# Expert bias as three bf16 parts on 96 rows, made in the banded stage

## The chip, the cores and the metric

One core of one Trainium2 chip runs the whole program. The metric is the device time of one execution in microseconds (us). The granted clock of TensorE has two levels here, 1.2 and 2.4 GHz.

## What is computed

One encoder block on x of 1024 tokens and 1024 columns, all float32, followed by a mixture of experts. What matters here is the second half:

```
logits = xt @ w_router + b_router
top_val, top_idx = lax.top_k(logits, TOP_K)          # 4 of 32 experts
gates = jax.nn.softmax(top_val, axis=-1)
...
gu = xb @ w_gate_up[e] + b_gate_up[e]                # 1024 -> 2 x 1024, bias 32 x 2048
gate = jnp.minimum(gu[:, :D_FF], SWIGLU_LIMIT)
up = jnp.clip(gu[:, D_FF:], -SWIGLU_LIMIT, SWIGLU_LIMIT)
act = (up + 1.0) * (gate * jax.nn.sigmoid(SWIGLU_ALPHA * gate))
y = act @ w_down[e] + b_down[e]
```

Each token's four rows y, times its gates, are added to the residual x; a last RMSNorm gives the output. Before it stand an input projection, stick-breaking attention, sliding window attention and an output projection.

## The kernel before

Float32 products are made of parts. A weight or an activation is split in a high part, rounded to fp32r (ScalarE), and a low part, the rest (VectorE), and TensorE does three fp32r matmuls, high x high, high x low and low x high.

**Stages.** First the norm and its transposes, then the input projection together with stick-breaking attention, ending at about 374 us. Then the **banded stage**: sliding window attention in 32 steps, four to each of the eight tiles of 128 tokens, with the later work of each tile in the same loop at fixed steps behind it, as written out in `out_stage(step)` on VectorE and ScalarE and in `before_turn` and `after_values` on TensorE. `tile_at(step, n)` is the tile whose turn comes n steps after its first step, 4t + n. For tile t VectorE does at 4t + 7 the scaled rows (`mix_rows`, L1781), at 4t + 8 the low parts (`mix_low_part`, L1866), at 4t + 13 the residual (L1801), at 4t + 15 the normed row h2 (`normed`, L1811), at 4t + 18 the routing (L1818 to L1837), at 4t + 20 the places (L1844 to L1860). Beside it runs `band(u + 1)` (L1745, L1749), the scores of the next step, which ScalarE then exponentiates and TensorE turns (L924). Steps 32 to 48 are the tail, without attention.

GpSimd in that stage splits q (L712 to L715), adds the output bias to x (`x2_bias`, L722, at step 4t + 12), takes powers (L646) and writes records of the tokens to their experts' slots by indirect DMAs (L653). SP's queue, per tile t: load x of tile t (L566), then store the residual of tile t - 1 (L569) and h2 of tile t - 1 (L571), each after its semaphore. Behind tile 7 it stores the last two (L575, L577), **loads the bias twice** (L579), and the first weights (L525).

**The bias before.** b_gate_up, 32 experts by 2048 columns, lies on rows 0 to 31 and again on 32 to 63 of `bias_raw`. After the tables of items are started, VectorE adds 1 to the up half (L1934, the "+ 1" of the activation), ScalarE rounds it to fp32r (L1589) into `bias_hl`, VectorE clears rows 64 to 127 (L1973) and makes rows 32 to 63 the rest (L1975, `bias_done`). TensorE and ScalarE wait for `bias_done` before the loop. In the same stretch TensorE turns the first item's gathered rows (L1120), ScalarE makes `x_high` (L1496), VectorE `x_low` (L1969).

**The expert loop**, 33 items, each an expert and up to 192 of its tokens. The first 128 are the stationary operand. TensorE's order for an item: bias of gate and up (`expert_bias`, L1142, two matmuls for each half h of the hidden columns), 8 units of weights for h = 0, 8 for h = 1 (`hidden`, L1152), 8 of the down projection (L1174). A unit is 1024 weight columns, six matmuls of 512 columns. `pick` is a matrix with ones in the rows of the expert, made by GpSimd (`choose`, L766), so that pick x bias_hl puts the expert's bias on every token. Items with more than 128 tokens do the others in plain fp32, in narrow matmuls: 4 groups of 32 tokens' columns for up to 160 tokens, 2 of 64 for more. Their bias is the k = -1 of `over_hidden` (L1186):

```
bias = bias_f.rearrange("p (g h f) -> p h g f", g=2, h=2)
for k in range(-1, KT):
    for q in range(parts):
        lhs = pick_f[:, 0:m] if k < 0 else xo[:, k, 0:m]
        rhs = bias[:, h] if k < 0 else gu_w[:, h, k]
```

Weights are loaded by SP (L525 gate and up, 1 MB for two units; L549 down), refilled as soon as they are split and, in items with extra tokens, used by `over_hidden`. ScalarE makes high parts (L1519), VectorE low parts (L1995), five units ahead at most.

## Time and profile before

| what | value |
|---|---|
| median of 3 runs | 2077.31 us (2076.71 to 2078.88) |
| the profiled execution's own time | 2076.9 us |
| its span, first to last instruction | 2075.1 us |
| TensorE matmul busy | 1955.7 us (94%) |
| VectorE busy | 1579.5 us (76%) |
| ScalarE busy | 1397.3 us (67%) |
| GpSimd busy | 468.7 us (23%) |
| HBM read, written | 472.09 MB, 38.55 MB |
| mean granted TensorE clock | 0.974 of 2.4 GHz |

In the rows below PE is TensorE's matmuls, PEld its weight loads, DVE VectorE, ACT ScalarE, POOL GpSimd, SPq the queue of SyncE. A matmul's recorded time is from its start to its modelled end and overlaps the next one, so its cost is read from one start to the next. `128*32 128x256 f32 x8` is a stationary operand of 128 rows and 32 columns, 256 moving columns, eight instructions. L1186 is line 1186.

### The profile page before, as it was taken

Reading aid. Unit: us, or ns where it says so; the run is one execution under the profiler, and the core shown is the slowest. Engines: PE = TensorE matmul, PEld = TensorE weight load, DVE = VectorE, ACT = ScalarE, POOL = GpSimd, SP = SyncE. Lnnn points to the kernel's source line nnn. Section 1 sums busy time; section 2 is a strip of 40 time slices with the busy share of each in tenths; the row PEclk is TensorE's granted clock in tenths of the full one; section 3 lists DMA queues with packets and bytes.
Section 4 is the critical chain, followed back from the end, with each engine's and each line's share of the span. In section 5 each row is a group of like instructions: output and inputs, shape, how many; then the busy total and the mean of one; then the engine's idle time right before and its main releaser. Section 6 shows DMA issues by size and latency. Waiting matters only on the chain.

```text
span 2075.1 us, 38069 instructions
## 1 busy us (share of the span) xinstructions
PE 1955.7 (94%) x11383; PEld 1521.9 (73%) x11384; DVE 1579.5 (76%) x1990; ACT 1397.3 (67%) x1880; POOL 468.7 (23%) x625
## 2 busy tenths in 40 slices
PE   6989999799949999999999999999999999999994
PEld 5777777688737888877877777877876778576583
DVE  5667677778767899987987877976976878586596
ACT  4667768654316888876876766866875777475484
POOL 1222314556420111111111111111111111021023
PEclk9999999899969999999999999999999999999997
DMA  6110020221249999998998988998997999697695
GB/s 228 41 30 22 23 80 1 102 72 63 94 148 326 350 373 373 375 375 314 360 339 287 343 304 286 371 332 276 360 326 251 314 333 337 233 334 253 218 333 200
DMA packets 249636, 507.49 MB, mean 245 GB/s; under 512 B 44502, under 2 KB 61708, under 8 KB 249324
## 3 DMA queue, kind: packets, MB, share of 16 engines
q1 hardware_dynamic: 233948, 463.25, 62.7%
q0 software_dynamic: 15632, 43.53, 8.2%
q8 instruction: 31, 0.51, 0.1%
q14 instruction: 25, 0.20, 0.0%
HBM read 472.09 MB, written 38.55 MB: 246 GB/s over the span
## 4 chain that ended last, share of the span: by engine, by line
PE 77%; SPq 7%; DVE 5%; DMA 4%; issue 3%; ACT 3%; POOL 1%; ACTq 0%; POOLq 0%; DVEq 0%
PE bank L1152 29%; PE bank L1174 15%; PE bank L896 9%; PE bank L1186 7%; SPq L525 4%; PE bank L1203 3%; PE bank L1001 2%; PE bank L924 2%; SPq L536 2%; PE bank L978 1%; PE bank L1142 1%; PE bank L1120 1%; PE bank L1158 1%; DMA slot_in<-slot_rows 1%; PE bank L966 1%
## 5 line engine op out<-in xcount | busy, mean ns | idle before, releaser
L1995 DVE TENSOR_TENSOR w_low<-gu_w,w_high 128x1024 fp32r<-128x1024 f32 x528 | 618.5, 1220 | 222.8 <-ACT w_high L1519 213.4
L1519 ACT CAST w_high<-gu_w 128x1024 fp32r<-128x1024 f32 x528 | 537.7, 1051 | 240.2 <-PE bank L1174 124.2
L1152 PE MATMUL bank<-w_high,x_high 128*128 128x512 f32 x1056 | 415.9, 394 | 2.2 <-DVE w_low L1995 2.2
L1152 PE MATMUL bank<-w_high,x_low 128*128 128x512 f32 x1056 | 413.7, 392 | 0.0
L1152 PE MATMUL bank<-w_low,x_high 128*128 128x512 f32 x1056 | 413.1, 391 | 0.0
L1995 DVE TENSOR_TENSOR w_low<-dn_w,w_high 128x1024 fp32r<-128x1024 f32 x264 | 315.5, 1226 | 24.2 <-ACT w_high L1519 19.3
L1519 ACT CAST w_high<-dn_w 128x1024 fp32r<-128x1024 f32 x264 | 270.0, 1050 | 24.8 <-PE bank L1152 19.5
L1152 PEld LDWEIGHTS bank<-w_high,x_high 128*128 128x128 f32 x1056 | 198.9, 188 | 45.9 <-DVE w_low L1995 3.0
L1152 PEld LDWEIGHTS bank<-w_high,x_low 128*128 128x128 f32 x1056 | 198.8, 188 | 42.8
L1152 PEld LDWEIGHTS bank<-w_low,x_high 128*128 128x128 f32 x1056 | 198.9, 188 | 42.0
L1174 PE MATMUL bank<-w_high,act_high 128*128 128x512 f32 x528 | 215.5, 408 | 0.0
L1174 PE MATMUL bank<-w_high,act_low 128*128 128x512 f32 x528 | 206.7, 391 | 0.0
L1174 PE MATMUL bank<-w_low,act_high 128*128 128x512 f32 x528 | 206.0, 390 | 0.0
L794 POOL DMA_INDIRECT residual_rows<-y_sb,scat_idx x33 | 55.8, 1691 | 535.0 <-ACT y_sb L1527 275.2
L1186 PE MATMUL bank<-gu_w,xo 128*32 128x256 f32 (+1 forms) x1536 | 129.0, 415 | 0.0
L1174 PEld LDWEIGHTS bank<-w_high,act_high 128*128 128x128 f32 x528 | 99.1, 188 | 34.5 <-issue 10.9
L896 PE MATMUL bank<-hT_high,in_high 128*128 128x512 f32 x288 | 120.6, 419 | 0.0
L896 PE MATMUL bank<-hT_low,in_high 128*128 128x512 f32 x288 | 116.5, 404 | 0.0
L896 PE MATMUL bank<-hT_high,in_low 128*128 128x512 f32 x288 | 115.8, 402 | 0.0
L1174 PEld LDWEIGHTS bank<-w_high,act_low 128*128 128x128 f32 x528 | 99.1, 188 | 21.8
L779 POOL COPY gather_idx<-slot_in 128x4 int32 (+1 forms) x34 | 17.6, 519 | 422.9 <-DMA slot_in<-slot_rows 422.9
L1174 PEld LDWEIGHTS bank<-w_low,act_high 128*128 128x128 f32 x528 | 99.4, 188 | 17.7
(247 smaller groups left out, 3104.1 us busy)
## 6 DMA issues: line engine op xcount, KB each, us to landing
gu_w<-in_w_gate_up SPq DMA_DIRECT2D x528, 512.0 KB, 10.5
dn_w<-in_w_down SPq DMA_DIRECT2D x132, 1024.0 KB, 17.2
w_st<-in_w_in SPq DMA_DIRECT2D x14, 512.0 KB, 3.8
xt<-in_x SPq DMA_DIRECT2D x8, 512.0 KB, 10.2
wo_sb<-in_w_out SPq DMA_DIRECT2D x2, 2048.0 KB, 10.4
x<-in_x SPq DMA_DIRECT2D x8, 512.0 KB, 4.2
residual_rows<-x SPq DMA_DIRECT2D x8, 512.0 KB, 2.6
h_rows<-h SPq DMA_DIRECT2D x8, 512.0 KB, 2.8
```

Of the source, the lines that this page charges most:

```text
L525: sp.dma_start(gu_w[:, h, k:k + 2, g, :], w_gate_up[e, P * k:P * k + 2 * P, c0:c0 + HALF] .rearrange("(k p) f -> p k f", p=P)).then_inc(d_ ...
L536: sp.dma_start(slot_in[rows:rows + m, bass.ds(8 * n + (8 + 2 * k), 2)], slots[e, bass.ds(first + at, m), word:word + 2]).then_inc(landed, 16)
L794: pool.indirect_dma_start(acc_dram.rearrange("r (q d) -> (r q) d", q=parts), bass.IndirectOffsetOnAxis(ap=scat_idx[:, k:k + 1].bitcast(U32 ...
L896: mm = pe.matmul(bank[:, proj_bank(n), :], a, b[:, k, cols], start=(r == 0), stop=(r == HALF_STEPS - 1))
L924: mm = pe.transpose(bank[:, 4 + g % 2, P * (b % 4):P * (b % 4) + P], src[:, P * b:P * b + P], ident)
L1001: mm = pe.matmul(bank[:, 2 + half, :], a, b[:, k, cols], start=first, stop=last)
L1152: mm = pe.matmul(bank[:, 2 * h + g, :], a[:, k, :], b, start=False, stop=last)
L1174: mm = pe.matmul(bank[:, 4 + half, :], a[:, j, :], b, start=first, stop=last)
L1186: mm = pe.matmul(over_view(parts)[m * q:m * q + m, h], lhs, rhs[:, :, w * q:w * q + w], start=(k < 0), stop=(k == KT - 1))
L1203: mm = pe.matmul(bank[m * q:m * q + m, 7, 0:n], overT[:, c0:c0 + m], dn_w[:, j, n * q:n * q + n], start=(j == 0), stop=(j == FT - 1))
L1519: act.copy(w_high[:, u % RING, :], src).then_inc(high_ready, 1)
L1995: dve.tensor_tensor(w_low[:, u % RING, :], raw, w_high[:, u % RING, :], ALU.subtract).then_inc(split_ready, 1)
```

## The change

The bias is made as three bf16 parts (the rounded value, the rounded rest, the rounded rest of that), on rows 0 to 31, 32 to 63 and 64 to 95 of `bias_b`. `bias_raw` is now 128 rows of 512 columns: row 32j + e has columns 512j to 512j + 511 of expert e, so columns of up are rows 64 to 127. Seven VectorE steps, one at the end of each step 24 to 30 of the banded stage (`BIAS_STEP` = 24), add 1 to rows 64 to 127, round, subtract, round, subtract, round, and clear rows 96 to 127 of `bias_b`. SP loads the four blocks of 64 KB at its t = 2, and at its t = 6 copies the parts with 12 transfers of 32 KB from `bias_part` to `bias_b`. `pick` is bf16 with ones in three rows. The old preparation between the stages, its loads and its waits are gone; TensorE waits for the 12 landings instead.

```diff
@@ -52,6 +52,7 @@
 LAST = BAND * (NT - 1) + 20
+BIAS_STEP = BAND * 5 + 4
@@ -132,7 +133,7 @@
         scat_idx = keep("scat_idx", [P, 8], I32)
-        pick = keep("pick", [P, P], F32R)
+        pick = keep("pick", [P, P], BF16)
         assert o <= 18 * KB, o
@@ -207,12 +208,13 @@
         w_low = at("w_low", [P, RING, D], F32R, W + 4 * RING * KB)
-        bias_raw = at("bias_raw", [2 * NE, 2 * FF], F32, W + 16 * KB)
         overT = at("overT", [P, HALF], F32, M + 28 * KB)
-        bias_hl = at("bias_hl", [P, 2 * FF], F32R, Z)
+        bias_raw = kb("bias_raw", [P, HALF], F32, 100)
+        bias_part = at("bias_part", [P, 3, HALF], BF16, Z)
+        bias_b = at("bias_b", [P, 2 * FF], BF16, Z + 4 * KB)
@@ -302,7 +304,7 @@
         pool_step, over_step = sem("pool_step"), sem("over_step")
-        bias_up, bias_high, bias_done = sem("bias_up"), sem("bias_high"), sem("bias_done")
+        bias_step, d_bias_b = sem("bias_step"), sem("d_bias_b")
         slots_ready, pick_ready = sem("slots_ready"), sem("pick_ready")
@@ -569,14 +571,21 @@
                     sp.dma_start(h2_dram[(t - 1) * P:t * P, :], h2[:]).then_inc(d_h2, 16)
+                if t == 2:
+                    for j in range(4):
+                        sp.dma_start(bias_raw[NE * j:NE * j + NE, :], b_gate_up[:, HALF * j:HALF * j + HALF]).then_inc(d_bias, 16)
+                if t == 6:
+                    sp.wait_ge(bias_step, 7)
+                    for m in range(3):
+                        for j in range(4):
+                            sp.dma_start(bias_b[NE * m:NE * m + NE, HALF * j:HALF * j + HALF],
+                                         bias_part[NE * j:NE * j + NE, m, :]).then_inc(d_bias_b, 16)
             sp.wait_ge(op_ready, NT)
             sp.dma_start(h2_dram[(NT - 1) * P:NT * P, :], h2[:]).then_inc(d_h2, 16)
-            for r in range(2):
-                sp.dma_start(bias_raw[NE * r:NE * r + NE, :], b_gate_up).then_inc(d_bias, 16)
             for s in range(1, 4):
@@ -763,7 +772,7 @@
             def choose(e):
-                pool.tensor_copy(pick[0:2 * NE, :], cst[0:2 * NE, bass.ds(e + C_PICK, 1)].to_broadcast([2 * NE, P])
+                pool.tensor_copy(pick[0:3 * NE, :], cst[0:3 * NE, bass.ds(e + C_PICK, 1)].to_broadcast([3 * NE, P])
                                  ).then_inc(pick_ready, 1)
@@ -1139,7 +1148,7 @@
                     c0 = FF * g + HALF * h
-                    pe.matmul(bank[:, 2 * h + g, :], pick[:], bias_hl[:, c0:c0 + HALF], start=True, stop=False)
+                    pe.matmul(bank[:, 2 * h + g, :], pick[:], bias_b[:, c0:c0 + HALF], start=True, stop=False)
@@ -1174,14 +1183,12 @@
-            pick_f, bias_f = pick[:].bitcast(F32), bias_hl[:].bitcast(F32)
             def over_hidden(i, h, parts):
                 m, w = P // parts, HALF // parts
-                bias = bias_f.rearrange("p (g h f) -> p h g f", g=2, h=2)
+                bias = bias_b.rearrange("p (g h f) -> p h g f", g=2, h=2)
                 for k in range(-1, KT):
                     for q in range(parts):
-                        lhs = pick_f[:, 0:m] if k < 0 else xo[:, k, 0:m]
+                        lhs = pick[:, 0:m] if k < 0 else xo[:, k, 0:m]
                         rhs = bias[:, h] if k < 0 else gu_w[:, h, k]
@@ -1223,7 +1230,7 @@
             pe.wait_ge(tables_ready, 2)
-            pe.wait_ge(bias_done, 1)
+            pe.wait_ge(d_bias_b, 16 * 12)
             n_items = pe.value_load(item_tab[0:1, 3 * MAX_ITEMS:3 * MAX_ITEMS + 1], min_val=NE, max_val=MAX_ITEMS - 1)
@@ -1582,16 +1589,12 @@
             load_tables(SILU_TABLES)
-            act.wait_ge(d_bias, 32)
-            act.wait_ge(bias_up, 1)
             act.wait_ge(lg_ready, NT)
             act.wait_ge(d_h2, 16 * NT)
-            act.copy(bias_hl[0:2 * NE, :], bias_raw[:]).then_inc(bias_high, 1)
             act.wait_ge(tables_ready, 1)
             act.wait_ge(tables_ready, 2)
-            act.wait_ge(bias_done, 1)
             n_items = act.value_load(item_tab[0:1, 3 * MAX_ITEMS:3 * MAX_ITEMS + 1], min_val=NE, max_val=MAX_ITEMS - 1)
@@ -1680,7 +1683,7 @@
             dve.wait_ge(setup_pe, 2)
-            dve.memset(pick[:].bitcast(F32), 0.0)
+            dve.memset(pick[:], 0.0)
             chain(dve.tensor_copy(in_bias[:], bank[:, 3, 0:CHUNKS]))
@@ -1859,6 +1862,22 @@
+            def bias_terms(n):
+
+                if n == 0:
+                    dve.wait_ge(d_bias, 64)
+                    up = bias_raw[2 * NE:P, :]
+                    dve.tensor_scalar(up, up, 1.0, None, ALU.add).then_inc(bias_step, 1)
+                elif n == 6:
+                    dve.memset(bias_b[3 * NE:P, :], 0.0).then_inc(bias_step, 1)
+                elif n % 2 == 1:
+                    dve.wait_ge(bias_step, n)
+                    dve.tensor_copy(bias_part[:, n // 2, :], bias_raw[:]).then_inc(bias_step, 1)
+                else:
+                    dve.wait_ge(bias_step, n)
+                    dve.tensor_tensor(bias_raw[:], bias_raw[:], bias_part[:, n // 2 - 1, :], ALU.subtract
+                                      ).then_inc(bias_step, 1)
+
             def mix_low_part(t, part):
@@ -1904,6 +1923,8 @@
                     routing(t)
+                if BIAS_STEP <= step < BIAS_STEP + 7:
+                    bias_terms(step - BIAS_STEP)
@@ -1930,8 +1951,6 @@
             dve.sem_inc(tables_ready, 1)
-            dve.wait_ge(d_bias, 32)
-            dve.tensor_scalar(bias_raw[:, FF:2 * FF], bias_raw[:, FF:2 * FF], 1.0, None, ALU.add).then_inc(bias_up, 1)
@@ -1970,10 +1989,6 @@
             further_items()
-            dve.memset(bias_hl[2 * NE:P, :].bitcast(F32), 0.0)
-            dve.wait_ge(bias_high, 1)
-            dve.tensor_tensor(bias_hl[NE:2 * NE, :], bias_raw[NE:2 * NE, :], bias_hl[NE:2 * NE, :], ALU.subtract
-                              ).then_inc(bias_done, 1)
             x_low_part(0)
@@ -2082,7 +2097,7 @@
     c[:, C_CODE:C_CODE + NE] = np.arange(NE)
-    c[:, C_PICK:C_PICK + NE] = (row[:, None] % NE == np.arange(NE)[None, :]) & (row[:, None] < 2 * NE)
+    c[:, C_PICK:C_PICK + NE] = (row[:, None] % NE == np.arange(NE)[None, :]) & (row[:, None] < 3 * NE)
     return c
```

## Rows read from the trace of the kernel before

**Rows 1.** Busy time by stretch: us, PE, PEld, DVE, ACT, POOL busy (x), PEclk, DMA, GB/s.

```profile
440.00:580.00 140.00, 132.23 (x833) 113.75 (x833) 104.86 (x309) 57.33 (x151) 75.96 (x90) 1.00 0.21 74
604.00:626.00 22.00, 4.39 (x19) 3.16 (x19) 16.91 (x32) 6.18 (x7) 6.20 (x8) 0.50 0.38 108
700.00:1000.00 300.00, 296.49 (x1519) 239.56 (x1518) 263.83 (x258) 239.44 (x267) 49.38 (x55) 1.00 1.02 362
1000.00:1300.00 300.00, 300.00 (x2009) 231.87 (x2008) 236.43 (x234) 215.88 (x245) 46.78 (x47) 1.00 0.93 320
```

**Rows 2.** Waits of TensorE's matmuls, 640 to 2020 us: total, times, longest.

```profile
PE bank L1120 <- DMA xg<-h_rows,gather_idx: 3.0, 3, 1.0
```

**Rows 3.** Timeline of TensorE, narrow stretch of 32 columns: start, us, engine, line.

```profile
639.30 0.64 PE L1186 MATMUL bank<-bias_hl,pick 128*32 128x256 f32 x8
639.76 3.64 PE L1186 MATMUL bank<-gu_w,xo 128*32 128x256 f32 x64
```

**Rows 4.** Timeline of TensorE, narrow stretch of 64 columns.

```profile
1534.20 1.08 PE L1186 MATMUL bank<-bias_hl,pick 128*64 128x512 f32 x4
1535.11 7.04 PE L1186 MATMUL bank<-gu_w,xo 128*64 128x512 f32 x32
```

**Rows 5.** Timeline of TensorE, an item without extra tokens, its first half.

```profile
711.61 0.64 PE L1142 MATMUL bank<-bias_hl,pick 128*128 128x512 f32 x2
712.09 0.40 PE L1152 MATMUL bank<-w_high,x_high 128*128 128x512 f32 x1
...
723.05 0.64 PE L1142 MATMUL bank<-bias_hl,pick 128*128 128x512 f32 x2
```

**Rows 6.** Instructions that read `pick`: duration ns min/median/max, first and last start.

```profile
L1186 PE MATMUL bank<-bias_hl,pick x192: 379/403/643, 639.3 to 1939.8; 128*32 128x256 f32 x160, 128*64 128x512 f32 x32
L1142 PEld LDWEIGHTS bank<-bias_hl,pick x132: 186/189/333, 622.4 to 2014.5; 128*128 128x128 f32 x132
```

**Rows 7.** Timeline of TensorE, ranks of the last tile, a bf16 product.

```profile
600.06 0.37 PE L1031 MATMUL bank<-mask_b,ones_b 128*128 128x32 bf16 x7 [3.44 <-DVEq L1837]
600.25 0.10 PEld L1032 LDWEIGHTS bank<-mask_b,tri_b 128*128 128x128 bf16 x1
```

**Rows 8.** Busy time by stretch, two items without extra tokens; columns as in rows 1.

```profile
711.61:747.37 35.76, 35.76 (x166) 29.44 (x165) 33.15 (x33) 29.96 (x33) 5.98 (x7) 1.00 1.05 374
855.63:892.48 36.85, 35.84 (x166) 29.33 (x164) 33.16 (x33) 29.97 (x33) 6.03 (x7) 1.00 1.05 375
```

**Rows 9.** Timeline of VectorE, banded stage.

```profile
514.83 3.39 DVE L1811 SCALAR_TENSOR_TENSOR h<-x,st,ffn_bc 128x1024 f32<-128x1024 f32 x1
...
530.41 0.48 DVE L1745 CUSTOM_DVE_ANT_0 tC<-bank,swbias,sinks_bc 128x256 f32<-128x256 f32 x1 [2.37 <-PE bank L939]
...
538.50 1.28 DVE L1811 SCALAR_TENSOR_TENSOR h<-x,st,ffn_bc 128x1024 f32<-128x1024 f32 x1
```

**Rows 10.** Timeline of GpSimd, banded stage.

```profile
514.44 2.70 POOL L722 TENSOR_TENSOR x<-x,bout_bc 128x1024 f32<-128x1024 f32 x1
```

**Rows 11.** Timeline of TensorE, banded stage.

```profile
520.49 0.63 PE L924 MATMUL bank<-cst,tC 128*128 128x128 f32 x4 [1.12 <-DVE mix_low L1866]
...
538.56 1.03 PE L924 MATMUL bank<-cst,o_row 128*128 128x128 f32 x8
```

**Rows 12.** Timeline of SP and GpSimd, end of the banded stage.

```profile
558.81 0.37 SPq L566 DMA_DIRECT2D x<-in_x  x1
...
568.79 2.40 POOL L722 TENSOR_TENSOR x<-x,bout_bc 128x1024 f32<-128x1024 f32 x1
```

**Rows 13.** Timeline of VectorE between the stages.

```profile
604.66 0.69 DVE L1934 TENSOR_SCALAR bias_raw<-bias_raw 64x1024 f32<-64x1024 f32 x1 [0.16 <-DVE item_tab L1931]
...
615.51 1.76 DVE L1973 MEMSET bias_hl<- 64x2048 f32 x1 [0.60 <-DVE item_tab L1962]
617.29 2.28 DVE L1975 TENSOR_TENSOR bias_hl<-bias_raw,bias_hl 32x2048 fp32r<-32x2048 f32 x1
619.98 1.49 DVE L1969 TENSOR_TENSOR x_low<-bank,x_high 128x512 fp32r<-128x512 f32 x2 [0.41 <-ACT x_high L1496]
```
## The prediction

> **What bounds the kernel now.** First the busy time by stretch [rows 1]. In the expert loop (700 to 2020 us) TensorE is busy all the time at the full granted clock, 2.4 GHz; the DMA engines are near full too, and VectorE is the next busiest. In the banded stage (440 to 580) TensorE is busy 132 of 140 us. Between the two, 604 to 626, nothing is full and the granted clock is 0.50, that is 1.2 GHz: a chain of latencies. Then the waits of the loop: TensorE's longest in total is 3.0 us, for gathered rows [rows 2]. So a microsecond of TensorE in the loop is worth a microsecond of the kernel, as long as DMA and VectorE keep up, and one taken from VectorE between the stages is worth only what its chain is late.
>
> The reader then needs the bias matmuls, a small part of that loop. They are of two kinds [rows 6]: 132 full ones (L1142, four in each of 33 items), and 192 narrow ones (L1186) in items with more than 128 tokens. The forms give the numbers: 160 of 32 columns, eight to a half of an item, so 20 halves of 10 items; 32 of 64 columns, four to a half, so 8 halves of 4 items. The code writes four (or two) narrow matmuls in a half, so an fp32 matmul is two instructions.
>
> **Term 1, narrow bias in bf16.** The eight instructions of a 32-column half start at 639.30 and the next k at 639.76: 0.46 us. The eight k behind them take 3.64 together, 0.45 each with the tail [rows 3]. For 256 columns at 2.4 GHz one pass is 0.107 us, so a half's bias is four passes, with the four column groups side by side. A 64-column half: 1534.20 to 1535.11, 0.91 us for 512 columns [rows 4], again four passes of 0.213. A bf16 matmul is one instruction: seven matmuls are seven in the row of the ranks [rows 7]. How long a bf16 narrow one takes no row shows. It cannot be under one pass (0.107 and 0.213), and at worst it is as long as one of the two fp32 instructions it replaces (0.23 and 0.455). I take 0.12 and 0.24, near one pass, because the fp32 rows fit passes to a few hundredths. That saves 0.34 x 20 = 6.8 and 0.67 x 8 = 5.4: **-12.2 us**, bounds -8.2 (0.23 x 20 + 0.455 x 8) and -12.6. All of it is TensorE time in items where nothing else is full, since DMA is at 0.93 over such stretches [rows 1].
>
> **Term 2, full bias in bf16.** A pair of them runs from 711.61 to 712.09, 0.24 us each; the 48 fp32r neighbours behind them take 712.09 to 723.05, 0.228 each [rows 5]. So fp32r is already one pass, and bf16 gains only what is over the columns. Bounds: no gain, and 0.213 us, which is 0.028 x 132 = 3.7. I take the neighbours' pitch: 0.012 x 132 = 1.6. The weight load falls from 189 ns [rows 6] to the 0.10 us of the bf16 one [rows 7]. It is hidden in a stream, and shows where TensorE comes out of a branch, that is before at most two pairs in each of 14 items: 28 x 0.09, 2.5 us at most. I take a quarter, 0.6. Some items without extra rows are held by DMA: 36.85 instead of 35.76 us with the DMA share over 1 [rows 8]. There the gain is lost, 0.2 us. **-2.0 us**, bounds 0 and -6.2.
>
> The Trainium skill, page "TensorE: Matmul & The Clock Gate", section "Back-to-back issue gap", gives about 216 ns for an isolated bf16 matmul of 512 columns and about 131 ns in a sustained stream. No row here shows a bf16 one. By 216 ns this term would be about -3.3, by 131 ns about -14.5. The second is a rival below.
>
> **Term 3, the start of the loop.** Removed: VectorE's plus one (0.69), memset (1.76) and subtract (2.28), ScalarE's copy, two loads on SP, and the wait of TensorE and ScalarE for the result. The subtract ended at 619.57, yet VectorE's next instruction ran only at 619.98, after idling for ScalarE's x_high, which follows the gather [rows 13]. So the preparation was hidden behind records, slots and gather. The plus one lies before the item tables, which gather does not need, and the second tables are ready before PE wants them. **-0.1 us**, bounds 0 and -0.7 (if the records are written a little sooner).
>
> **Term 4, the banded stage.** Seven VectorE steps, at steps 24 to 30, each at the end of its step. Prices by the nearest rows: plus one on 512 columns, half of 0.69 and some, 0.4; three casts of 512 columns 0.4 each (same kind; at worst 0.69); two subtracts 0.69 each (a quarter of 2.28 is 0.57, plus start); memset of 2048 bf16 elements, below 1.76, I take 0.9 [rows 13]. Sum 3.9 us. By where they fall: the first and last cast (steps 25, 29) stand before a wait of VectorE for TensorE's scores, 2.37 us at 530.41 [rows 9], and cost nothing; plus one and second subtract (24, 28) come one step ahead of it and are taken up there too. Without that wait each would cost itself. The first subtract (26) lengthens a row of VectorE work that leads to L1811, which took 3.39 us instead of 1.28 [rows 9], while GpSimd ran L722 from 514.44 to 517.14 [rows 10]: it started late whatever VectorE did, and absorbs the subtract. The second cast (27) comes right behind it, before the mix that TensorE awaited 1.12 us at 520.49 [rows 11]: +0.6 with some stall. The memset (30) delays L1781 (o_row), the input of the turn that TensorE began at 538.56 without idling [rows 11]; the two were just in step: +0.9, and TensorE is the chain from there. A DMA part: four loads (SP, t = 2) and, at t = 6, 12 small transfers in front of the load of the last tile of x. The semaphore they wait for is long up (step 30 against 35). An issue is 0.37, so 12 are 4.4 us: the load goes out at 563.2 instead of 558.81, and GpSimd wants it at 568.79 [rows 12]. Hidden; with slower issues it would cost GpSimd about 2 us before a residual that waits for TensorE's last projection anyway. What the queue holds behind it (two stores and the first weights) comes later than 566. TensorE's new wait on the 12 landings, over by about 570, ends 50 us before use. **+1.6 us**, bounds -1 (a collision that happens to go away) and +4 (both subtracts and a slow memset on the path).
>
> The Trainium skill, page "SBUF — State Buffer", speaks against this part: whichever of a GpSimd instruction and a VectorE one in a 2-port mode or with two SBUF inputs starts first has the shared ports for its whole length. The two L1811 rows agree. By it the casts and the subtracts can each draw such a stall; it is the second rival.
>
> Moving the pick to 96 rows of bf16 changes a GpSimd copy of some 0.3 us that nobody waits for: nothing.
>
> **Sum.** -12.2 - 2.0 - 0.1 + 1.6 = -12.7 us. Against the profiled execution's own 2076.9 (span 2075.1, 1.8 around it) that is 2064.2; the median of the runs is 0.4 above that execution, so **2064.6 us**. All bounds together reach from -20.5 (2056.8) to -4.2 (2073.1). Chance **0.80**.
>
> **Rivals.** (a) The bf16 column groups do not run side by side. For: no row shows them in bf16. Against: the fp32 ones do, and the 64-column fp32 ones as well. Then a half costs 4 x 0.107 or 2 x 0.213, 0.43, and term 1 is 0.03 x 20 + 0.48 x 8 = 4.4: -4.9, 2072.4. Chance 0.07. (b) Slower: port stalls in the banded stage. Place: the seven steps; price: each draws the 2.1 us of L1811 (3.39 - 1.28) and its own length, 7 x 2.1 + 3.9 = 18.6 us on the path. With -14.3 from the rest that is +4.3, 2081.6. It decides once the stage grows by over 14.3. Against: GpSimd's long instruction comes once in a tile, and four steps stand before waits. Chance 0.04. (c) DMA takes over: TensorE's gain is handed to waits for weights. For: 36.85 us items, share 0.93 to 1.02. Against: no wait for weights in the loop, and in items with extra rows the share is lower. Half of the loop's 14.2 lost: -5.6, 2071.7. Chance 0.05. (d) A full bf16 matmul hides behind its neighbours and takes half of its 0.24: 0.12 x 132 = 15.8 instead of 2.0, -26.5, 2050.8. Against: the columns alone are 0.213 us at 2.4 GHz, and no pitch of 512 columns in the rows is lower. The skill's 131 ns is the rule behind it; the trace does not bear it out. Chance 0.02. The last 0.02 is for what I have not seen, of either sign.
>
> **Numbers.** The likeliest case gives the time. The range 2060 to 2072 takes in (c); it leaves out (a), (b), (d), the unseen 0.02 and the far ends of the bounds, to which I give 0.05: 0.2 in all. A measurement tells about 0.2%, 4.2 us, from no change, so faster means under 2073.2: the forecast, most of (c), half of (a), and (d), 0.89. Same 0.08, slower 0.03.
>
> **What would show it.** Right: a 32-column half's bias at about 0.12 us before the next k, a 64-column one at 0.24; items with 32-column halves shorter by 0.7 to 0.8 us, with 64-column ones by 1.4; items without extra rows by under 0.15; the stretch from the end of the banded stage to the first bias matmul unchanged; that matmul itself 1 to 2 us later than 622.4. Wrong: bias halves of 0.2 us or more; waits of TensorE for w_low or of ScalarE for weights in the loop; more L1811-like stalls between 495 and 545.

## Result and profile after

The changed kernel took 2060.72 us (median of four runs, 2057.52 to 2061.89) against 2077.01 us of the kernel before (median of four, 2075.18 to 2078.88). The ratio is 0.9926, 95% interval 0.9907 to 0.9944: faster, clear of noise, by 12 to 19 us, which is less than 1%.

| what | before | after |
|---|---|---|
| profiled execution's own time | 2076.9 us | 2061.89 us |
| its span | 2075.1 us | 2060.1 us |
| TensorE matmul busy | 1955.7 us | 1932.2 us |
| VectorE busy | 1579.5 us | 1576.5 us |
| ScalarE busy | 1397.3 us | 1394.8 us |
| GpSimd busy | 468.7 us | 473.1 us |
| mean granted TensorE clock | 0.974 | 0.974 |

**Where the 15.0 us of the span went.** I cut both executions at the same instructions: VectorE's residual of a tile (L1801 before, L1804 after; tile 7's is the last), the first weight matmul of the expert loop (L1152, now L1161), the last of the down projection (L1174, now L1183), the end. Each entry is a difference of two starts.

| stretch | before | after | difference |
|---|---|---|---|
| start to residual 3 | 502.96 | 502.32 | -0.6 |
| residual 3 to residual 7 | 77.93 | 80.28 | +2.35 |
| residual 7 to first weight matmul | 44.95 | 44.97 | 0.0 |
| expert loop | 1412.76 | 1395.64 | -17.1 |
| end | 36.51 | 36.88 | +0.4 |

The first, third and last row differ more between executions of one kernel than between these two. In two more executions of the changed kernel tile 0's residual starts at 435.31 and 432.64 (434.37 here), the third row is 45.4 and 45.9, and the end takes 35.9 and 37.5. The other two rows are the change; the loop took 1396.6 and 1395.3 there.

**The narrow bias.** Timeline of TensorE in the changed kernel, a half of 32 columns; the rows answer to [rows 3].

```profile
641.41 0.29 PE L1193 MATMUL bank<-bias_b,pick 128*32 128x256 bf16 x4
641.53 3.63 PE L1193 MATMUL bank<-gu_w,xo 128*32 128x256 f32 x64
```

The same for a half of 64 columns, answering to [rows 4].

```profile
1527.31 0.41 PE L1193 MATMUL bank<-bias_b,pick 128*64 128x512 bf16 x2
1527.55 7.03 PE L1193 MATMUL bank<-gu_w,xo 128*64 128x512 f32 x32
```

From the start of the bias to the next k: 0.12 us where it was 0.46, and 0.24 where it was 0.91. Four column groups (or two) in bf16 are one instruction each, x4 instead of x8, and take one pass side by side.

**The full bias.** The instructions that read `pick`, answering to [rows 6].

```profile
L1151 PEld LDWEIGHTS bank<-bias_b,pick x132: 96/99/113, 624.6 to 1999.2; 128*128 128x128 bf16 x132
L1193 PE MATMUL bank<-bias_b,pick x96: 283/283/404, 641.4 to 1924.9; 128*32 128x256 bf16 x80, 128*64 128x512 bf16 x16
L1151 PE MATMUL bank<-bias_b,pick x66: 379/379/634, 625.0 to 1999.4; 128*128 128x512 bf16 x66
```

The weight load takes 99 ns (it took 189). In this execution only 66 of the 132 full matmuls have a record, while all 132 loads have one. So the pair must be read from its neighbours, and TensorE's busy time of this execution is a little too low. Timeline of TensorE, the same item as [rows 5]:

```profile
712.55 0.39 PE L1183 MATMUL bank<-w_high,act_low 128*128 128x512 f32 x1
713.00 0.38 PE L1151 MATMUL bank<-bias_b,pick 128*128 128x512 bf16 x1
713.03 0.58 PE L1161 MATMUL bank<-w_high,x_high 128*128 128x512 f32 x1
713.45 0.40 PE L1161 MATMUL bank<-w_low,x_high 128*128 128x512 f32 x1
```

and of the kernel before, the rows on both sides of the pair of [rows 5]:

```profile
711.37 0.40 PE L1174 MATMUL bank<-w_high,act_low 128*128 128x512 f32 x1
...
712.32 0.40 PE L1152 MATMUL bank<-w_low,x_high 128*128 128x512 f32 x1
```

From the last matmul of the down projection to the second one of the weights it was 712.32 - 711.37 = 0.95 us and is 713.45 - 712.55 = 0.90. A second execution of the changed kernel has a record of all 132, and its starts give 0.90 again (0.903 unrounded, from 712.17):

```profile
712.40 0.60 PE L1151 MATMUL bank<-bias_b,pick 128*128 128x512 bf16 x2
712.66 0.58 PE L1161 MATMUL bank<-w_high,x_high 128*128 128x512 f32 x1
713.08 0.40 PE L1161 MATMUL bank<-w_low,x_high 128*128 128x512 f32 x1
```

Here too the first weight matmul is noted 0.03 us behind a bias matmul and its successor 0.42 later, so that spacing is not the missing record; only the sum over both is used below.

One of an item's two pairs stands elsewhere: in the 14 items with extra tokens the second pair comes directly behind the narrow matmuls of the first half. Timeline of TensorE at such a pair, item 12, of the kernel before and then of the changed kernel's second execution:

```profile
1115.40 0.72 PE L1142 MATMUL bank<-bias_hl,pick 128*128 128x512 f32 x2
...
1116.19 0.40 PE L1152 MATMUL bank<-w_low,x_high 128*128 128x512 f32 x1
```

```profile
1114.88 0.61 PE L1151 MATMUL bank<-bias_b,pick 128*128 128x512 bf16 x2
...
1115.55 0.40 PE L1161 MATMUL bank<-w_low,x_high 128*128 128x512 f32 x1
```

From the start of the pair to the second weight matmul it is 0.79 and then 0.67 us: 0.12 saved. The same stretch of a pair in a stream was 712.32 - 711.61 = 0.71 and is 713.08 - 712.40 = 0.68; with its start, 0.95 to 0.90, it saves 0.05.

**By items** (from the second weight matmul of one to that of the next; the last of the 33 has no next):

| items | before | after | difference |
|---|---|---|---|
| no extra tokens, e.g. item 2 | 35.76 | 35.63 | -0.11 to -0.21; item 7 +0.06 |
| 32-column halves, e.g. item 8 | 48.01 | 47.13 | -0.88 to -0.90, nine items |
| 64-column halves, items 22, 29 | 60.23 | 58.69 | -1.54 |
| 64-column halves, items 27, 30 | 59.38 | 57.84 | -1.54 |
| item 0, has 32-column halves | 50.11 | 49.62 | -0.49 |

Items 0 and 7 are no measure: between executions of the changed kernel item 0 takes 48.81 to 49.62 and item 7 38.36 to 40.15. The others repeat within 0.07 us, most of them within 0.02.

**The banded stage.** Timeline of VectorE in the changed kernel, around [rows 9].

```profile
511.05 1.17 DVE L1878 TENSOR_TENSOR bias_raw<-bias_raw,bias_part 128x512 f32<-128x512 f32 x1 [0.16 <-DVE gates L1839]
...
513.74 0.74 DVE L1784 SCALAR_TENSOR_TENSOR o_row<-o_sb,st,mix_bc 128x512 f32<-128x512 f32 x1
514.40 2.84 DVE L1784 SCALAR_TENSOR_TENSOR o_row<-o_row,st,mix_bc 128x512 f32<-128x512 f32 x1
517.16 1.41 DVE L1814 SCALAR_TENSOR_TENSOR h<-x,st,ffn_bc 128x1024 f32<-128x1024 f32 x1
518.50 0.62 DVE L1875 CAST bias_part<-bias_raw 128x512 bf16<-128x512 f32 x1
...
538.63 0.91 DVE L1872 MEMSET bias_b<- 32x1024 uint32 x1 [0.40 <-DVE gates L1839]
```

Of the kernel before, the rows ahead of the first of [rows 9]:

```profile
512.89 0.89 DVE L1781 SCALAR_TENSOR_TENSOR o_row<-o_sb,st,mix_bc 128x512 f32<-128x512 f32 x1
513.70 1.21 DVE L1781 SCALAR_TENSOR_TENSOR o_row<-o_row,st,mix_bc 128x512 f32<-128x512 f32 x1
```

Timeline of GpSimd and of TensorE after; the first answers to [rows 10].

```profile
513.79 2.90 POOL L731 TENSOR_TENSOR x<-x,bout_bc 128x1024 f32<-128x1024 f32 x1
```

```profile
517.29 1.06 PE L933 MATMUL bank<-cst,o_row 128*128 128x128 f32 x4 [1.74 <-DVE o_row L1784]
...
519.01 0.63 PE L1010 MATMUL bank<-wo_high,mix_low 128*128 128x512 f32 x1
519.44 0.63 PE L1010 MATMUL bank<-wo_high,mix_high 128*128 128x512 f32 x1
```

The reader is to see three things. The subtract (with its start, 1.35 us) makes both rows of o_row later, while GpSimd's bias addition is where it was: this execution runs 0.65 us ahead here, so 513.79 is 514.44 of before. Now it stands ahead of the second o_row row, not ahead of h. That row takes 2.84 us instead of 1.21, and h 1.41 instead of 3.39. The stall has not grown, it has moved to a row that TensorE wants, and TensorE waits 1.74 us. Not all of that is lost: the wait of 1.12 us for mix_low that followed [rows 11] is 0.17 in the changed kernel's second execution, since TensorE comes there later. And the fp32r matmuls behind it start 0.43 us apart (519.01, 519.44), where they are 0.23 apart elsewhere. Busy time by stretch of this execution, columns as in [rows 1]:

```profile
496.00:516.00 20.00, 19.24 (x132) 17.03 (x132) 16.34 (x55) 10.76 (x31) 12.66 (x17) 1.00 0.16 55
516.00:520.00 4.00, 2.71 (x9) 2.32 (x10) 3.96 (x8) 0.80 (x2) 3.52 (x4) 0.67 0.15 61
520.00:524.00 4.00, 4.00 (x27) 3.50 (x26) 3.72 (x14) 0.00 (x0) 0.00 (x0) 0.90 0.68 207
```

The granted clock is 1.00 up to 516 and 0.67 over the next 4 us, in which TensorE idled for 1.74: part of that stretch ran at 1.2 GHz.

At step 30 the clearing (538.63) comes ahead of o_row, and the turn of [rows 11], which began without idling, waits:

```profile
540.46 1.32 PE L933 MATMUL bank<-cst,o_row 128*128 128x128 f32 x8 [0.44 <-DVE o_row L1784]
```

**SP's queue.** Timeline of SP after, answering to [rows 12], and of GpSimd.

```profile
561.11 8.46 SPq L581 DMA_DIRECT2D bias_b<-bias_part  x12
569.67 0.53 SPq L568 DMA_DIRECT2D x<-in_x  x1
```

```profile
574.30 3.08 POOL L731 TENSOR_TENSOR x<-x,bout_bc 128x1024 f32<-128x1024 f32 x1 [3.22 <-DMA x<-in_x]
```

The 12 transfers took 0.70 us each to issue. The load of x goes out at 569.67 instead of 558.81, and GpSimd, which did its addition at 568.79, waits 3.22 us for it.

### The profile page after: what moved, and what is told of

Same layout as the page of the kernel before. It is cut to its first block, busy times and chain, and to the rows that moved or that the text cites. A ratio compares the mean times of both kernels' runs of the same rounds, so it can differ in the third digit from the quotient of the medians.

```text
span 2060.1 us, 37826 instructions
## 1 busy us (share of the span) xinstructions
PE 1932.2 (94%) x11221; PEld 1498.2 (73%) x11288; DVE 1576.5 (77%) x1994; ACT 1394.8 (68%) x1879; POOL 473.1 (23%) x625
## 4 chain that ended last, share of the span: by engine, by line
PE 83%; DVE 5%; DMA 3%; SPq 3%; ACT 3%; issue 3%; POOL 0%; ACTq 0%; POOLq 0%; DVEq 0%
PE bank L1161 33%; PE bank L1183 17%; PE bank L905 9%; PE bank L1193 6%; PE bank L1210 3%; PE bank L1010 3%; PE bank L933 2%; PE bank L987 1%; PE bank L1129 1%; PE bank L1167 1%; SPq L527 1%; PE bank L1151 1%; PE bank L975 1%; SPq L538 1%; DMA wo_sb<-in_w_out 1%
## 5 line engine op out<-in xcount | busy, mean ns | idle before, releaser
L1161 PE MATMUL bank<-w_high,x_high 128*128 128x512 f32 x1056 | 428.3, 406 | 1.9 <-DVE w_low L2010 1.9
L1161 PE MATMUL bank<-w_high,x_low 128*128 128x512 f32 x1056 | 412.9, 391 | 0.0
L1161 PE MATMUL bank<-w_low,x_high 128*128 128x512 f32 x1056 | 412.6, 391 | 0.0
L1161 PEld LDWEIGHTS bank<-w_high,x_high 128*128 128x128 f32 x1056 | 199.1, 189 | 49.6 <-DVE w_low L2010 2.9
L1161 PEld LDWEIGHTS bank<-w_high,x_low 128*128 128x128 f32 x1056 | 198.9, 188 | 42.7
L1161 PEld LDWEIGHTS bank<-w_low,x_high 128*128 128x128 f32 x1056 | 199.3, 189 | 39.5
L1183 PE MATMUL bank<-w_high,act_high 128*128 128x512 f32 x528 | 215.4, 408 | 0.0
L1183 PE MATMUL bank<-w_high,act_low 128*128 128x512 f32 x528 | 206.3, 391 | 0.0
L1183 PE MATMUL bank<-w_low,act_high 128*128 128x512 f32 x528 | 206.2, 390 | 0.0
L1183 PEld LDWEIGHTS bank<-w_high,act_high 128*128 128x128 f32 x528 | 99.1, 188 | 34.6 <-issue 15.0
L1183 PEld LDWEIGHTS bank<-w_high,act_low 128*128 128x128 f32 x528 | 99.1, 188 | 21.7
L1183 PEld LDWEIGHTS bank<-w_low,act_high 128*128 128x128 f32 x528 | 99.4, 188 | 17.7
```

The costliest lines, as they stand in the source:

```text
L1161: mm = pe.matmul(bank[:, 2 * h + g, :], a[:, k, :], b, start=False, stop=last)
L1183: mm = pe.matmul(bank[:, 4 + half, :], a[:, j, :], b, start=first, stop=last)
```

## Experiments

Each kernel was timed in turn with the kernel before on the same chip; its ratio is to that. Experiments 1 and 2 ran on one chip, 3 to 5 on a second and 6 on a third. Where a doubled or shifted piece shows in single rows, the verdict rests on the profile.

**1. Every full bias matmul done twice, in both kernels** (the first of each two is overwritten by the second). The edit in the kernel before:

```diff
-                    pe.matmul(bank[:, 2 * h + g, :], pick[:], bias_hl[:, c0:c0 + HALF], start=True, stop=False)
+                    for last in (True, False):
+                        pe.matmul(bank[:, 2 * h + g, :], pick[:], bias_hl[:, c0:c0 + HALF], start=True, stop=last)
```

and the same with `bias_b` in the changed one.

> The kernel before with every full bias matmul (fp32r, L1142) done twice, the first result overwritten: 132 more. My theory: TensorE bounds the loop and one costs 0.23 to 0.24 us, so 30 to 32 us longer than before. Rival, that these matmuls lie beside other work: clearly less than 30.

> The changed kernel with every full bias matmul (bf16) done twice: 132 more. My theory, from the items that got 0.13 us shorter with four of them: one costs 0.215 us, 28.4 us over the changed kernel's 2060.7, so 2089. Rival, that the loop's gain beyond the narrow matmuls comes from elsewhere: the same addition as in the kernel before, 30 to 32, 2091 to 2093. Rival, that bf16 hides behind its neighbours: under 20, below 2081.

Measured: before-twice 2097.64 us, ratio 1.0109 (1.0089 to 1.0129); after-twice 2086.08, 1.0048 (1.0030 to 1.0066). The loop takes 1436.86 and 1420.61 us, that is 24.1 and 25.0 more than with single ones (1412.76, 1395.64). Less than expected in both. One reason is common, and the theories lacked it: items 5 to 7, in which TensorE waited for gathered rows, absorb the added matmuls (item 7 takes 38.30 us before, 37.28 doubled; 38.36 and 37.25 after). All items but 0 and 5 to 7 grow by 0.8 to 1.0 us in both kernels, so the added matmuls do not lie beside other work there. In an undisturbed item without extra tokens four of them cost 0.83 us in fp32r (item 2, 35.76 to 36.59) and 0.95 in bf16 (35.63 to 36.58); in one with extra tokens 0.90 and 0.91 (item 8). Directly, from the last matmul of the down projection to the second one of the weights, two added ones take 1.40 - 0.95 = 0.45 us in fp32r and 1.34 - 0.90 = 0.44 in bf16. The timeline of TensorE with doubled bf16 ones:

```profile
710.53 0.39 PE L1184 MATMUL bank<-w_high,act_low 128*128 128x512 f32 x1
710.76 1.04 PE L1152 MATMUL bank<-bias_b,pick 128*128 128x512 bf16 x4
```

Four starts lie 1.04 - 0.38 = 0.66 us apart, 0.22 each; the fp32r pair of [rows 5] has 0.24. No full matmul hides behind its neighbours in either type, so rival (d) with 0.12 is out. With four in place of two, bf16 is ahead by 0.06 us (1.40 against 1.34), with two by 0.05: the gain of a pair is mostly not one per matmul. The rest of an item moves the other way. The 46 fp32r matmuls from the second to the 48th of item 2's first half take 10.50 us before and 10.45 with four fp32r bias matmuls ahead of them; after, 10.46 and then 10.50 with four bf16 ones. That is why the item of both doubled kernels takes the same, 36.58 and 36.59, and the items with extra tokens do not (48.91 against 48.04, where the narrow bias is 0.67 of it).

**2. Every narrow bias matmul done twice, in both kernels** (overwritten again).

```diff
-                for k in range(-1, KT):
+                for k in (-2, *range(-1, KT)):
...
-                                       start=(k < 0), stop=(k == KT - 1))
+                                       start=(k < 0), stop=(k in (-2, KT - 1)))
```

> The kernel before with the narrow fp32 bias of each half done twice. My theory, four passes each: 20 x 0.43 + 8 x 0.85 = 15.4 us longer than before, about 2092.5.

> The changed kernel with the narrow bf16 bias of each half done twice. My theory, one pass each with the column groups side by side: 20 x 0.11 + 8 x 0.21 = 3.9 us over the changed kernel's 2060.7, about 2064.6. Rival, groups one behind the other: 20 x 0.43 + 8 x 0.43 = 12 us, 2072.7.

Measured: before-twice 2090.51 us, ratio 1.0070 (1.0052 to 1.0088); after-twice 2064.62, 0.9952 (0.9934 to 0.9969). The loop grows by 16.1 us before and 3.5 after. The kernel grew by 15.4 us before and by 3.9 over the changed kernel's 2060.7 after, both as expected. By items: a 32-column one grows by 0.90 before (0.45 a half) and 0.26 after (0.13 a half), a 64-column one by 1.75 and 0.48 (0.24 a half). The timeline of the doubled narrow bias after:

```profile
638.00 0.40 PE L1193 MATMUL bank<-bias_b,pick 128*32 128x256 bf16 x8
638.23 3.63 PE L1193 MATMUL bank<-gu_w,xo 128*32 128x256 f32 x64
```

Two rounds of four matmuls take 0.23 us, where eight in a row, one after another, would take 8 x 0.107 = 0.86 of columns alone. Rival (a) is out: the groups run side by side in bf16 too, and by the items the saving is 0.45 - 0.13 in a half of 32 columns and 0.87 - 0.24 in one of 64.

**3. The banded part alone**, in the kernel before: the seven steps and the 16 transfers, on tiles that nobody reads, while the bias is made as before.

```diff
+                if t == 2:
+                    for j in range(4):
+                        sp.dma_start(dead_raw[NE * j:NE * j + NE, :], b_gate_up[:, HALF * j:HALF * j + HALF]).then_inc(d_rel, 16)
...
+                if BIAS_STEP <= step < BIAS_STEP + 7:
+                    bias_terms(step - BIAS_STEP)
```

> The kernel before, its own preparation and loop untouched, with all of the new work in the banded stage added on tiles that nobody uses (four loads, seven VectorE steps, 12 transfers). My theory: the banded stage gets 1.7 to 2.5 us longer and so does the kernel. Rival, that the stage hides them and the changed kernel's later start is chance: 0 to 0.5.

Measured: 2075.74 us against 2076.12, ratio 1.0002 (0.9993 to 1.0011). The time cannot tell 1.5 us; the starts can. From residual 3 to residual 7 it takes 79.41 us instead of 77.93: +1.5, a little under the 1.7 to 2.5 expected. Its rows show the same moved stall:

```profile
510.37 2.90 POOL L735 TENSOR_TENSOR x<-x,bout_bc 128x1024 f32<-128x1024 f32 x1
```

```profile
510.97 2.85 DVE L1795 SCALAR_TENSOR_TENSOR o_row<-o_row,st,mix_bc 128x512 f32<-128x512 f32 x1
```

```profile
513.88 0.66 PE L937 MATMUL bank<-cst,o_row 128*128 128x128 f32 x4 [1.72 <-DVE o_row L1795]
```

**4. The old preparation left out**, in the kernel before, with nothing in its place: the loads, plus one, copy, clearing and subtract are gone, and `bias_hl` is cleared once. This kernel leaves the expert bias out of the computation.

```diff
-            act.copy(bias_hl[0:2 * NE, :], bias_raw[:]).then_inc(bias_high, 1)
...
-            dve.memset(bias_hl[2 * NE:P, :].bitcast(F32), 0.0)
-            dve.wait_ge(bias_high, 1)
-            dve.tensor_tensor(bias_hl[NE:2 * NE, :], bias_raw[NE:2 * NE, :], bias_hl[NE:2 * NE, :], ALU.subtract
-                              ).then_inc(bias_done, 1)
```

> The kernel before without the preparation between the stages: no loads, plus one, rounding or subtract, the bias tile is only cleared (at step 45), so the bias is left out of the result; the loop's instructions are the same. My theory, that it was hidden behind records, slots and gather: within 0.7 us of the kernel before. Rival, that its removal is part of the gain: 2 to 4 us faster.

Measured: 2075.80 us, ratio 0.9999 (0.9990 to 1.0008). From residual 7 to the first weight matmul: 45.28 us against 44.95. Timeline of VectorE between the stages in this kernel, answering to [rows 13]:

```profile
611.52 0.18 DVE L1957 CAST item_tab<-ov 128x22 int32<-128x22 f32 x1
617.82 1.47 DVE L1964 TENSOR_TENSOR x_low<-bank,x_high 128x512 fp32r<-128x512 f32 x2 [6.12 <-ACT x_high L1494]
```

VectorE is done 6 us before x_high, and nothing starts sooner for it: the preparation was hidden, as expected.

**5. The changed kernel again, and its seven steps later.** In the late version all seven stand together at step 45, in the stretch where VectorE waits for the logits of the last tile, and the 12 transfers go out behind the first weights.

```diff
-BIAS_STEP = BAND * 5 + 4
+BIAS_STEP = LAST - 3
...
-                if BIAS_STEP <= step < BIAS_STEP + 7:
-                    bias_terms(step - BIAS_STEP)
+                if step == BIAS_STEP:
+                    for n in range(7):
+                        bias_terms(n)
```

> The changed kernel again, unchanged, as the measure for the others of this call: 2057 to 2062 us, 14 to 18 below the kernel before.

> The changed kernel with all seven VectorE steps at step 45, where VectorE waited 5.8 us for TensorE in the kernel before, and the 12 transfers behind the first weights. My theory, that the seven steps cost about 2.4 us between steps 26 and 30 and are free in that wait: 1.5 to 2.5 us faster than the changed kernel, 2058.5. Rival, that the place does not matter: the same time as the changed kernel.

Measured: the changed kernel 2059.93 us, ratio 0.9920 (0.9907 to 0.9934); the late version 2057.92, 0.9912 (0.9899 to 0.9926). Timeline of VectorE in the late version:

```profile
588.26 0.42 DVE L1869 TENSOR_SCALAR bias_raw<-bias_raw 64x512 f32<-64x512 f32 x1 [0.16 <-DVE record L1860]
588.72 0.43 DVE L1874 CAST bias_part<-bias_raw 128x512 bf16<-128x512 f32 x1
589.18 0.69 DVE L1877 TENSOR_TENSOR bias_raw<-bias_raw,bias_part 128x512 f32<-128x512 f32 x1
...
591.81 0.91 DVE L1871 MEMSET bias_b<- 32x1024 uint32 x1 [0.27 <-issue]
593.88 0.19 DVE L1820 TENSOR_TENSOR lg<-bank,rb_bc 128x32 f32<-128x32 f32 x1 [1.15 <-PE bank L1031]
```

After all seven VectorE still waits 1.15 us for TensorE (5.78 in the kernel before). Residual 3 to 7 takes 77.92, as before, and residual 7 to the first weight matmul 45.05.

**6. Both once more, and two versions between them.** One moves the clearing alone from step 30 to step 29; the other does the steps only next to VectorE's waits for TensorE: one at 24, two at 25, four at 29.

```diff
-                if BIAS_STEP <= step < BIAS_STEP + 7:
-                    bias_terms(step - BIAS_STEP)
+                for n in {0: (0,), 1: (1, 2), 5: (3, 4, 5, 6)}.get(step - BIAS_STEP, ()):
+                    bias_terms(n)
```

> The changed kernel once more, as the measure for this call: 2058 to 2062 us; from residual 3 to residual 7 (steps 25 to 41) 79.4 to 80.3 us, against 77.9 in the kernel before.

> The kernel with all seven steps at step 45 once more, to narrow its interval: 1.5 to 2.4 us faster than the changed kernel of this call; residual 3 to residual 7 in 77.9 us, as in the kernel before. Rival, place does not matter: no difference between the two.

> The changed kernel with the memset alone moved, from step 30 to step 29, before the wait. My theory: residual 4 to residual 5 shorter by the memset's 0.9 us (21.8 to 20.9), the rest as in the changed kernel. Rival, that the memset was hidden at step 30 too: no difference.

> The changed kernel with the seven VectorE steps all at steps 24, 25 and 29 (one, two and four of them), that is before VectorE's two waits of 2 us for TensorE. My theory, that what a step costs is set by whether a wait stands behind it: residual 3 to residual 7 in 77.9 to 78.5 us. Rival, that it is the amount of VectorE work between steps 24 and 30 whatever its place: 79.4 to 80.3.

Measured: changed kernel 2060.44 us, ratio 0.9928 (0.9915 to 0.9941); late 2058.15, 0.9917 (0.9904 to 0.9929); clearing moved 2057.49, 0.9918 (0.9906 to 0.9931); at the waits 2057.20, 0.9917 (0.9904 to 0.9930). The intervals overlap, so these ratios rank nothing by themselves. That the late version lay 2.0 us below the changed kernel in experiment 5 and 2.3 here agrees with the starts (1.5 to 2.4 in the stage). The other two lay 3.0 and 3.2 below it, more than their stretches show (1.0 to 2.0 and 1.3 to 2.3 from residual 0 to 7), so a part of that is not explained. Stretches between residuals of all these kernels, one execution each:

| kernel | 0 to 3 | 3 to 4 | 4 to 5 | 5 to 6 | 6 to 7 | 0 to 7 |
|---|---|---|---|---|---|---|
| before | 67.85 | 23.86 | 20.93 | 17.67 | 15.47 | 145.8 |
| banded part alone | 67.98 | 24.89 | 21.78 | 17.92 | 14.81 | 147.4 |
| changed | 67.95 | 25.83 | 21.79 | 17.85 | 14.81 | 148.2 |
| changed, again | 67.97 | 24.88 | 21.78 | 17.93 | 14.81 | 147.4 |
| changed, third | 68.01 | 25.85 | 21.77 | 17.94 | 14.81 | 148.4 |
| clearing at 29 | 67.98 | 24.93 | 20.92 | 17.70 | 14.81 | 146.3 |
| at the waits | 69.23 | 23.09 | 21.04 | 17.93 | 14.81 | 146.1 |
| late | 67.94 | 23.88 | 20.92 | 17.68 | 15.44 | 145.9 |
| late, again | 68.00 | 23.86 | 20.92 | 17.71 | 15.47 | 146.0 |

Columns say which step costs what. 3 to 4: the moved stall, +1.0, and +1.95 in two of the executions (the two doubled versions of the changed kernel, which have the same steps, took 24.89 each). 4 to 5: the clearing, +0.86, gone when it stands one step earlier, before a wait of VectorE. 6 to 7: -0.66 wherever the 12 transfers stand ahead of the load of x, and nothing where they don't. At the waits the stretch 3 to 4 is shorter by 0.8 than before, and the one ahead of it is longer by 1.4. The 1.4 are not the steps': up to residual 3 this kernel does what the changed one does, and its fp32r matmuls start 0.58 and 0.42 us apart at 496.74 and 497.32. Busy time by stretch there:

```profile
496.00:500.00 4.00, 4.00 (x16) 3.40 (x16) 2.59 (x10) 3.72 (x12) 2.43 (x3) 0.72 0.02 4
```

The granted clock fell in this execution ahead of residual 3 and TensorE came late to it, so VectorE had time to spare. From residual 3 to 7 it took 76.9 us, outside both expectations (77.9 to 78.5 and 79.4 to 80.3). The second o_row row still started behind GpSimd's addition (511.24 against 510.63) and took 2.85 us, but TensorE waited only 0.44 us for it. So this execution does not show whether the steps at 24 and 25 are free; that the last four are at 29 agrees with the stretch 4 to 5 (21.0).

The second value of 3 to 4 goes with the granted clock. Busy time by stretch at the same place of the changed kernel's second execution, again as in [rows 1]:

```profile
516.00:520.00 4.00, 2.26 (x15) 1.81 (x14) 4.00 (x3) 1.76 (x4) 3.81 (x4) 1.00 0.01 2
520.00:524.00 4.00, 3.73 (x26) 3.02 (x25) 3.78 (x16) 0.00 (x0) 0.67 (x1) 1.00 0.76 264
```

and of its third:

```profile
516.00:520.00 4.00, 4.00 (x13) 3.27 (x12) 3.93 (x11) 0.59 (x1) 1.96 (x2) 0.59 0.57 181
```

TensorE waited for o_row 1.74 us in the second execution and 1.75 in the third. In the one the clock stayed at 2.4 GHz, in the other it fell to 1.2 GHz for a while. With the clearing at 29 TensorE waited 1.79 us, the clock stayed at 1.00 and the stretch took 24.93. What decides between the two these runs do not show.

The -0.66 has its own rows. VectorE in the kernel before, while GpSimd ran its addition from 568.79 for 2.40 us [rows 12]:

```profile
569.20 2.03 DVE L1826 TENSOR_SCALAR eqm<-lg,top 128x32 f32<-128x32 f32 x1
```

and in the changed one, whose addition ran only at 574.30:

```profile
571.57 0.24 DVE L1829 TENSOR_SCALAR eqm<-lg,top 128x32 f32<-128x32 f32 x1
...
576.45 0.98 DVE L1853 TENSOR_TENSOR codes<-codes,mask_b 128x32 f32<-128x32 f32 x1
```

The late load of x spared the routing of tile 6 a stall of 1.8 us, 0.66 of which reaches the next residual; in the late version a row of 2.03 us (at 566.36) is back.

## Why the prediction was right, and where it was not

Forecast 2064.6 us, 2060 to 2072; measured 2060.7. The profiled execution was forecast at 2064.2 and took 2061.9. The direction and the likeliest case hold, and the median lies 0.7 us inside the lower end of the range; one term was too small by more than half, and one mechanism was told wrong and came out near its size. Three signs went a little beyond what the prediction wrote for them: items with 32-column halves got 0.88 us shorter (0.7 to 0.8), those with 64-column ones 1.54 (1.4), and items without extra tokens up to 0.21 (under 0.15).

**Term 1, -12.2: right.** The rows give 0.12 and 0.24 us, as taken. A half became 0.34 shorter in 32 columns and 0.67 in 64 (experiment 2 gives 0.45 - 0.13 and 0.87 - 0.24 by another way): 20 x 0.34 + 8 x 0.67 = 12.2 us.

**Term 2, -2.0: right in sign, mis-sized.** What is left of the loop's 17.1 us is 4.9. The step that failed is "I take the neighbours' pitch", 0.012 us for each matmul or 0.024 for a pair, and nothing for the matmuls behind it. Three things were measured in its place. A pair in a stream costs 0.05 us less (0.95 to 0.90); that is 51 pairs, 2.3 us from the unrounded 0.045. A pair directly behind narrow matmuls costs 0.12 us less (0.79 to 0.67); that is 14 pairs, 1.6 us. Of these, 14 x 0.07 = 1.0 us is more than pairs in a stream save. By its place and size (189 to 99 ns) that is the weight load where TensorE comes out of a branch, for which the text had 0.6; no run tests it alone. Last, the fp32r matmuls behind the pairs, from the second to the 48th of each half, got shorter by 1.5 us in the whole loop, a term that the sum did not have. Together 5.4, of which waits, for gathered rows and in item 0, take back 0.5 or so.

How much of the 0.05 us is the bf16 matmul itself is known in part: in a row of four they start 0.22 us apart and the added fp32r ones took 0.45 / 2 = 0.23, so two matmuls give 0.01 to 0.02 of it. The Trainium skill, page "TensorE: Matmul & The Clock Gate", section "Back-to-back issue gap", has about 216 ns for an isolated matmul of 512 columns: the bf16 ones in a row agree (0.22). Its 131 ns for a sustained stream does not hold here, neither for the bf16 matmuls nor for the fp32r stream around them (0.23).

Where the rest of the 0.05 us lies, and why the fp32r matmuls behind run a little slower or faster by what stood ahead of them (10.45 to 10.50 us for 46 in experiment 1), stays open.

**Term 3, -0.1: right.** From residual 7 to the first weight matmul it takes 44.95 us before, 45.0, 45.4 and 45.9 in three executions of the changed kernel, and 45.28 with the preparation left out: no gain shows. The cover was the wait for x_high, 5.8 us now.

**Term 4, +1.6: the size right, the reason half wrong.** Measured +1.5 in the commoner case and +2.4 with the fallen clock, within -1 and +4. (Its two priced steps, 0.6 and 0.9, add to 1.5.) Prices where nothing disturbs: plus one 0.42, cast 0.42, subtract 0.69, clearing 0.91, all as taken; in their places the first subtract took 1.17 and the second cast 0.62. The clearing: +0.9, as forecast. Plus one: free (67.95 us from residual 0 to 3 against 67.85). The first cast has a wait of 2.03 us behind it (505.91), and the last one stands in the stretch 4 to 5, which is as before once the clearing is at 29: free. The +1.0 from residual 3 to 4 holds the moved stall, the second cast, for which the text had 0.6, and the second subtract; no undisturbed run tells them apart. The 0.2 us more from residual 5 to 6 have no step of their own.

The step that failed is "it started late whatever VectorE did, and absorbs the subtract", said of L1811. GpSimd's addition did start at its own time, but the subtract pushed another row of VectorE's under it. The stall is paid by whichever row comes first behind the start of GpSimd's instruction, and now that was o_row, on TensorE's path, instead of h, which could wait. The Trainium skill, page "SBUF — State Buffer", section "SBUF: two separate sides", says that between GpSimd and a VectorE instruction with two SBUF inputs the shared ports belong for the whole instruction to whichever starts first. The rows agree: o_row went from 1.21 to 2.84 us, h from 3.39 to 1.41. I had the rule and the rows, and used them only as a price per stall (rival b), not to ask which row would be next. Against that, -0.66 from the transfers was in the text only as a far end, "a collision that happens to go away".

**SP's queue: mis-sized, hidden all the same.** 12 issues were costed at 0.37 each, from a single load, 4.4 us; they took 0.70 each, 8.5 us. The branch for slower issues in the text had GpSimd 2 us late; its addition started 5.5 us later by the clock of the trace, 2.4 of it the lateness of the whole stage, and cost nothing, since the residual of the last tile waits for TensorE.

**The rivals.** (a) and (d) fell in experiments 1 and 2. (b) did happen once, not seven times, and where the clock stayed up the whole stretch around it lost 1.0 us and not 2.1. (c) is not seen: TensorE has no wait for weights in the loop after, and only items 0 and 7 kept less of the gain than their like, item 7 with a wait for gathered rows.

## What to carry to other kernels

Count passes: a small fp32 matmul on TensorE cost four here and three bf16 parts stacked along the contraction cost one, for the same columns. When a step is put into an engine that shares ports with another one's long instruction, list the rows in order and ask which of them will now stand behind the start of that instruction and who waits for it; a stall that was harmless can move to a row that matters without growing. Put such steps behind the last collision, in a wait that the profile shows: here, step 45, at no cost.

## What was not expected of the hardware

- A pair of full bf16 bias matmuls saved 0.05 us against an fp32r pair in a stream and 0.12 behind narrow matmuls, four of them only 0.06 in a stream; the fp32r matmuls behind them changed by up to 0.05 us in 46, in either direction.
- A wait of TensorE of 1.74 us left the granted clock at 1.00 in one execution of the changed kernel; in another it was followed by 0.67 over 4 us, and in a third, after 1.75 us, by 0.59; the 3-to-4 stretch then took 0.95 us more. In the kernel of experiment 6 with its steps at the waits a wait of 1.22 us was followed by 0.72.
- An issue on SP took 0.70 us in a row of 12 transfers of 32 KB, 0.37 for the load of x in the kernel before and 0.53 for the one behind the 12.
- Half of the records of the full bf16 matmuls are missing (66 of 132) in two of three executions of the changed kernel, the two in which the clock fell, with all their weight loads there; the third has all 132. With or without them the fp32r matmul behind is noted only 0.03 us after the bias matmul before it.
